# A two-block transformer on one core: scores two groups ahead of the transposes, and the window mask written into PSUM by ScalarE

## What is computed

```python
def first_block(x, ...):
    for l in range(DEPTH):                       # DEPTH = 2
        h = rmsnorm(x, norm_mix[l])
        proj = jnp.einsum('btd,de->bte', h, w_in[l])
        q, k, v, u, ug, ga, gb = jnp.split(proj, SPLITS, axis=-1)
        q = partial_rope(rmsnorm(q, q_norm[l]), cos, sin)     # 16 heads of 64
        k = partial_rope(rmsnorm(k, k_norm[l]), cos, sin)     # 2 heads of 64
        a_out = sliding_window_attention(q, k, v, sinks[l])
        c_out = conformer_conv(u, ug, conv_w[l], conv_b[l], conv_ln_g[l], conv_ln_b[l], w_conv_out[l])
        merged = jax.nn.sigmoid(ga) * a_out + jax.nn.sigmoid(gb) * c_out
        x = x + jnp.einsum('btd,de->bte', merged, w_out[l])
        h2 = rmsnorm(x, norm_ffn[l])
        gu = jnp.einsum('btd,df->btf', h2, w_gate_up[l])
        g, up = jnp.split(gu, 2, axis=-1)
        x = x + jnp.einsum('btf,fd->btd', jax.nn.silu(g) * up, w_down[l])

def sliding_window_attention(q, k, v, sinks):    # window 128, blocks of 128 queries see 256 keys
    s = jnp.einsum('bnqkgd,bnskd->bnkgqs', qb, kb) * scale
    s = jnp.where(mask, s, -jnp.inf)
    m = jnp.maximum(jnp.max(s, axis=-1, keepdims=True), sink)
    p = jnp.exp(s - m)
    p = p / (jnp.sum(p, axis=-1, keepdims=True) + jnp.exp(sink - m))
    o = jnp.einsum('bnkgqs,bnskd->bnqkgd', p, vb)
```

## Time and profile before

| | us |
|---|---|
| median of three runs | 2336.82 (2336.79 to 2336.86) |
| the profiled execution | 2334.86 |
| its span, first to last instruction | 2332.6 |
| PE busy | 2271.0 (97%) |
| DVE busy | 1137.1 (49%) |
| ACT busy | 993.5 (43%) |
| POOL busy | 981.8 (42%) |
| mean granted clock of TensorE | 0.993 of full speed |

### The profile page before, as it was taken

The page is one execution under the profiler, slowest core; times in us unless marked ns, Lnnn a source line. Parts: engine busy times, 40 slices in busy tenths (PEclk is TensorE's granted clock), DMA queues, the critical chain, the costliest instruction groups (busy, mean ns, idle before and its releaser), DMA issues.

```text
span 2332.6 us, 29198 instructions
## 1 busy us (share of the span) xinstructions
PE 2271.0 (97%) x10536; PEld 1791.9 (77%) x10560; DVE 1137.1 (49%) x1475; ACT 993.5 (43%) x1499; POOL 981.8 (42%) x453
## 2 busy tenths in 40 slices
PE   6989999999999999999999999999999999999999
PEld 5866678888888876678888888876777667888887
DVE  5876664222334785666222334647776443433300
ACT  4546643333223545744333213335535663444311
POOL 4962234444443882234444443432442113544442
PEclk9999999999999999999999999999999999999999
DMA  4321123333662221122333472322121002333332
GB/s 151 91 64 56 62 73 91 99 92 97 192 221 73 90 73 54 55 70 88 96 98 98 150 247 90 91 81 64 55 83 53 28 28 72 107 93 97 99 92 88
DMA packets 59842, 216.00 MB, mean 93 GB/s; under 512 B 6640, under 2 KB 6896, under 8 KB 59760
## 3 DMA queue, kind: packets, MB, share of 16 engines
q1 hardware_dynamic: 52272, 187.62, 26.0%
q10 hardware_dynamic: 7488, 27.27, 3.5%
HBM read 212.76 MB, written 2.10 MB: 92 GB/s over the span
## 4 chain that ended last, share of the span: by engine, by line
PE 88%; DVE 7%; ACT 4%; issue 2%; DMA 0%; SPq 0%; DVEq 0%; ACTq 0%
PE bank L1276 26%; PE bank L1278 25%; PE bank L1277 25%; PE bank L1732 1%; PE bank L1410 1%; PE bank L1289 1%; PE bank L1736 1%; PE bank L1470 1%; PE bank L1350 1%; PE bank L1450 1%; PE bank L1720 1%; PE bank L1345 1%; PE bank L1306 1%; ACT prob L479 1%; DVE root L749 1%
## 5 line engine op out<-in xcount | busy, mean ns | idle before, releaser
L307 POOL TENSOR_TENSOR wl<-raw,wh 128x1024 fp32r<-128x1024 f32 x351 | 855.7, 2438 | 1304.3 <-ACT wh L380 1304.1
L1276 PE MATMUL bank<-hh,wh 128*128 128x512 f32 x2024 | 816.3, 403 | 32.9 <-DVE hl L763 19.4
L1277 PE MATMUL bank<-hl,wh 128*128 128x512 f32 x2024 | 792.9, 392 | 0.0
L1278 PE MATMUL bank<-hh,wl 128*128 128x512 f32 x2024 | 792.8, 392 | 0.0
L380 ACT ACTIVATE wh<-raw 128x1024 fp32r<-128x1024 f32 x351 | 369.7, 1053 | 641.8 <-PE bank L1278 610.0
L1276 PEld LDWEIGHTS bank<-hh,wh 128*128 128x128 f32 x2024 | 383.1, 189 | 128.7 <-issue 28.6
L1277 PEld LDWEIGHTS bank<-hl,wh 128*128 128x128 f32 x2024 | 383.2, 189 | 86.3 <-issue 9.8
L1278 PEld LDWEIGHTS bank<-hh,wl 128*128 128x128 f32 x2024 | 382.7, 189 | 81.4
L1276 PE MATMUL bank<-ah,wh 128*128 (+1 forms) x528 | 208.0, 394 | 0.0
L1278 PE MATMUL bank<-ah,wl 128*128 (+1 forms) x528 | 207.0, 392 | 0.0
L1277 PE MATMUL bank<-al,wh 128*128 (+1 forms) x528 | 204.9, 388 | 0.0
(11 more groups left out here) (318 smaller groups left out, 2571.9 us busy)
## 6 DMA issues: line engine op xcount, KB each, us to landing
raw<-stream SPq DMA_DIRECT2D x351, 512.0 KB, 3.6
ada_w<-ada ACTq DMA_DIRECT2D x48, 512.0 KB, 4.6
x<-x_t ACTq DMA_DIRECT2D x4, 512.0 KB, 7.8
out_t<-x SPq DMA_DIRECT2D x8, 256.0 KB, 2.1
cst<-consts SPq DMA_DIRECT2D x1, 640.0 KB, 11.1
tmp<-masks SPq DMA_DIRECT2D x1, 320.0 KB, 11.3
par<-params SPq DMA_DIRECT2D x1, 253.0 KB, 4.6
cst<-consts SPq DMA_DIRECT2D x1, 224.0 KB, 8.0
```

The costliest lines, as they stand in the source:

```text
L307: nc.gpsimd.tensor_tensor(wl[:, slot, :], raw[:, raw_slot, :], wh[:, slot, :].bitcast(F32), ALU.subtract).then_inc(lo_ready, 1)
L1276: mm(dst, wh[:, slot, w], xh, start=start, stop=False)
L1277: mm(dst, wh[:, slot, w], xl, start=False, stop=False)
L1278: return mm(dst, wl[:, slot, w], xh, start=False, stop=stop)
```

## The change

The mask matmuls stay for groups 0 and 1. For groups 2 to 15 ScalarE copies `win_mask` into the two banks (`put_mask`, a new function, with a new semaphore `masked`), and the score matmuls add onto it. `put_mask(g + 4)` stands behind `exps(g + 2)`, which frees those banks.

Scores run two groups ahead: `scores(0)` and `scores(1)` stand in front of the loop, and in the loop `scores(g + 2)` stands behind the transposes of g. `maxima`, `exps` and `normalise` move with them. Gate tile 2 moves behind `scores(1)`, and gate tile 3 goes to bank 4. `SPLIT` goes from 16 to 20: four taps a layer move from VectorE to ScalarE and GpSimd. Of the layer norm the sum moves from group 4 to 3, variance from 7 to 8, root from 8 to 9, normalising and SiLU from 9 to 10, `ch` from 10 to 11, and `cl` from 10 to 12, where it now stands behind `gate`.

```diff
-        EARLY_GATES = 3
-        CO_FROM = 16 - EARLY_GATES
+        EARLY_GATES, AHEAD = 2, 2
+        CO_FROM = 13
-        TAPS_U, TAPS_Q = [2, 3, 4, 4, 4, 4], [4, 4, 3, 3, 5, 5, 5, 5]
-        SPLIT, LN_EARLY = 16, 2
+        TAPS_U, TAPS_Q = [2, 3, 4, 2, 4, 5], [5, 4, 3, 4, 5, 5, 5, 5]
+        SPLIT = 20
-        PRODUCTS_AT = {2: 3, C_K: 2, C_Q: 4, C_V: 2, C_GATE: 2, C_GATE + 1: 2, C_GATE + 2: 1}
+        PRODUCTS_AT = {2: 3, C_K: 2, C_Q: 4, C_V: 4, C_GATE: 2, C_GATE + 1: 3, C_GATE + 2: 2}
-        ADDS_AT = {2: 1, C_K: 2, C_V: 2, C_GATE: 2, C_GATE + 1: 2, C_GATE + 2: 2}
+        ADDS_AT = {2: 1, C_K: 2, C_V: 4, C_GATE: 2, C_GATE + 1: 4, C_GATE + 2: 2}
+        LN_SUM, LN_MEAN, LN_SQUARES, LN_VAR, LN_ROOT, LN_NORM, LN_HI, LN_REST = 3, 5, 6, 8, 9, 10, 11, 12
...
+                def put_mask(g):
+                    lo = P if group(g)[0] == 0 else 0
+                    b = 2 * (g % 2)
+                    act.wait_ge(exp_ready, 16 * l + g - 1)
+                    af(bank[:, b:b + 2, :].rearrange("p a (c d) -> p (a c) d", c=2)[:, :, lo:],
+                       win_mask[:, lo:2 * P].unsqueeze(1).to_broadcast([P, 4, 2 * P - lo]), ACT.Copy).then_inc(masked, 1)
...
                 exps(0)
+                exps(1)
+                put_mask(2)
+                put_mask(3)
+                gate(2)
+                products(C_GATE + 2)
+                gate(3)
...
-                    if g < 15:
-                        exps(g + 1)
+                    if g + AHEAD < 16:
+                        exps(g + AHEAD)
+                    if g + 2 * AHEAD < 16:
+                        put_mask(g + 2 * AHEAD)
...
-                    else:
-                        gate(g + EARLY_GATES)
+                    elif g:
+                        gate(g + 3)
...
-                taps(5)
-                gate(2, M_SWAP[7] % 4)
                 taps(len(own) - tapped[0])
...
                 maxima(0)
+                maxima(1)
+                gate(2, 6)
                 normalise(0)
+                normalise(1)
+                gate(3, 4)
                 for g in range(16):
...
-                    if g < 15:
-                        maxima(g + 1)
+                    if g + AHEAD < 16:
+                        maxima(g + AHEAD)
...
+                    if g + AHEAD < 16:
+                        normalise(g + AHEAD)
                     if g < CO_FROM:
-                        normalise(g + 1)
-                        if g == 12 - LN_EARLY:
+                        if g:
+                            gate(g + 3, 6)
+                        if g == LN_REST:
                             for t in range(CT):
                                 out_rest(t)
-                        gate(g + EARLY_GATES, 6)
                     else:
                         m = 2 * (g - CO_FROM)
                         gate_conv(m, 6)
...
-                        if g < 15:
-                            normalise(g + 1)
                         merge(m + 1)
...
                     if g >= 2:
-                        pe.wait_ge(exp_ready, 16 * l + g - 1)
-                    for kv in range(2):
-                        mm(bank[:, b + kv, :], ident_bf[:, :], win_mask[:, :], start=True, stop=False)
+                        pe.wait_ge(masked, 14 * l + g - 1)
+                    else:
+                        for kv in range(2):
+                            mm(bank[:, b + kv, :], ident_bf[:, :], win_mask[:, :], start=True, stop=False, skip_group_check=True)
...
                 scores(0)
-                pe.wait_ge(conv_ready, (CT - 1) * l + 2)
-                tile(c0 + C_GATE + EARLY_GATES, (c0 + C_GATE + EARLY_GATES) % RW, 6, hh, hl)
+                scores(1)
+                pe.wait_ge(conv_ready, (CT - 1) * l + 1)
+                tile(c0 + C_GATE + 2, (c0 + C_GATE + 2) % RW, 6, hh, hl)
                 pe.wait_ge(root_ready, ROOTS * l + 3)
+                tile(c0 + C_GATE + 3, (c0 + C_GATE + 3) % RW, 4, hh, hl)
...
-                    if g < 15:
-                        scores(g + 1)
                     if g >= CO_FROM:
                         out(2 * (g - CO_FROM), 6)
...
                     last.then_inc(turned, 1)
+                    if g + AHEAD < 16:
+                        scores(g + AHEAD)
```

More of the change, by code:

```diff
@@ L199, in build @@
         suffix_ready = stage("suffix_ready")
+        masked = stage("masked")
         v2_copied = stage("v2_copied")
@@ L500, in _ @@
                     af(prob_t[:, 1, :, :], bank[:, 5, :].rearrange("p (a b) -> p a b", a=4), ACT.Copy).then_inc(turned_out, 1)
-                    if g < 15:
-                        exps(g + 1)
-                    if g == 7 - LN_EARLY:
+                    if g + AHEAD < 16:
+                        exps(g + AHEAD)
+                    if g + 2 * AHEAD < 16:
+                        put_mask(g + 2 * AHEAD)
+                    if g == LN_MEAN:
                         for t in range(CT):
@@ L506, in _ @@
                             af(tmp[:, LN_TMP[t], :], conv[:, t, :], ACT.Square).then_inc(sq_ready, 1)
-                    if g == 9 - LN_EARLY:
+                    if g == LN_VAR:
                         act.wait_ge(var_out, l + 1)
                         af(root[:, :], tmp[:, 5, :], ACT.Sqrt).then_inc(root_ready, 1)
-                    if g == 11 - LN_EARLY:
+                    if g == LN_NORM:
                         for t in range(CT):
@@ L513, in _ @@
                             af(conv[:, t, :], conv[:, t, :], ACT.Silu, bias=par_l(l, "ln_b", t), scale=par_l(l, "ln_g", t)).then_inc(silu_ready, 1)
-                    if g == 12 - LN_EARLY:
+                    if g == LN_HI:
                         for t in range(CT):
@@ L946, in _ @@
                             tt(conv[:, t, :], conv[:, t, :], tmp[:, 5, :], ALU.add).then_inc(centred, 1)
-                    if g == 8 - LN_EARLY:
+                    if g == LN_SQUARES:
                         dve.wait_ge(sq_ready, l * SQ_LAYER + SQ_LN + CT)
@@ L951, in _ @@
                         tt(tmp[:, 0, :], tmp[:, 0, :], tmp[:, 4, :], ALU.add).then_inc(sq_used, CT)
-                    if g == 10 - LN_EARLY:
+                    if g == LN_ROOT:
                         invert(tmp[:, 5, :], root[:, :])
-                    if g == 11 - LN_EARLY:
+                    if g == LN_NORM:
                         for t in range(CT):
@@ L1389, in _ @@
                 pe.wait_ge(lin_free, m0 + M_SWAP[7] + 1)
-                tile(c0 + C_GATE + 2, (c0 + C_GATE + 2) % RW, M_SWAP[7] % 4, hh, hl)
                 def scores(g):
@@ L1410, in scores @@
                             last = mm(bank[:, b + kv, c + lo:c + 2 * P], q[half, 2 * j + i, n * P:n * P + P],
-                                      k[half, (n - 1) * P + lo:n * P + P], start=False, stop=i == 1)
+                                      k[half, (n - 1) * P + lo:n * P + P], start=False, stop=True, skip_group_check=True)
                     last.then_inc(scores_ready, 1)
@@ L1445, in _ @@
                     pe.wait_ge(probs_ready, 16 * l + g + 1)
-                    if g:
+                    if g == 0:
+                        pe.wait_ge(conv_ready, (CT - 1) * (l + 1))
+                    else:
                         pe.wait_ge(turned_out, 16 * l + g)
+                    if g == 1:
+                        pe.wait_ge(gate_free, 16 * l + 4)
                     for w in range(1 if n == 0 else 0, 2):
@@ L1451, in _ @@
                     last.then_inc(turned, 1)
-                    if g == 7 - LN_EARLY:
+                    if g + AHEAD < 16:
+                        scores(g + AHEAD)
+                    if g == LN_MEAN:
                         pe.wait_ge(mean_out, l + 1)
-                    if g == 9 - LN_EARLY:
+                    if g == LN_VAR:
                         pe.wait_ge(var_out, l + 1)
                     if 1 <= g < CO_FROM:
-                        pe.wait_ge(gate_free, 16 * l + g + EARLY_GATES)
-                        c = c0 + C_GATE + g + EARLY_GATES
+                        pe.wait_ge(gate_free, 16 * l + g + 3)
+                        c = c0 + C_GATE + g + 3
                         tile(c, c % RW, 6, hh, hl)
```

17 lines of the change are left out of this document (7 added, 10 removed).

## The result

The changed kernel is slower by 0.3%: 2345.06 us as the median of 14 runs, against 2338.93 for 14 runs of the kernel before beside them, a ratio of 1.003 (95% interval 1.0021 to 1.0038). That is 6.1 us; 4.2 were forecast. In time it is 2345.06 against 2341.0, inside both ranges. Half of the difference of 4.1 is the level of the kernel before (2338.9 here, 2336.8 in its first three runs), the rest is the change itself. Two executions of the kernel before, among those run beside the experiments, took 2855.57 and 5865.82 us; they are left out of the medians that follow.

A forecast was written before the change was run, and what follows sets the result against it. TensorE (PE), busy 2271.0 of 2332.6 us, was taken as the bound. Waits and clock added 9.5 us a layer, 19.0 in all, less 14.8 for masks: +4.2, so 2341.0 us, range 2330 to 2350 (the forecast's own 2335 to 2347).

The forecast's parts named there:

- output tile 1: Group 13: PE waits for gate_conv(0) behind the maxima and normalising of the scores just issued; 6.45 us, +6.2 a layer.
- start: First groups of a layer: PE waits 3.1 for group 0's values and 1.2 at gate tile 5; -1.4 a layer.
- groups 9 to 11: PE loses 0.7 to an even-chance GpSimd stall of row_max, then 1.8 to ScalarE's queue; together -0.1 a layer.
- output tile 0: Groups 12 to 13: PE waits 2.2 for the first `cl`, plus half a 1.4 stall; +2.9 a layer.
- less the waits before: The old kernel's six lines of PE waits in the attention stage, 20.1 us in all, 10.05 a layer.
- clock, less before: PE's clock halves behind the 6.45 wait at the second output tile, slowing the next tiles; +1.6 a layer, between 0 and 2.
- mask pairs: 28 pairs of mask matmuls leave PE, 14 a layer at 0.53 us each: 14.8 us less, 12.0 from below.
- Transposes behind values: On PE, eight transposes behind value matmuls take 0.85 us as behind scores, at no cost; upper end 4.7 us.
- rival 3: Transposes behind the values take 1.04, so 4.7 us of the 14.8 come back: 2345.7; chance 0.12.
- The mask write: ScalarE's 28 added mask copies: spacing 0.95 us, upper end 1.3, hidden except where ScalarE has a queue.
- Rival 1: Middle waits vanish: gate, mean, variance and first output tile are never waited for; -10 us, 2327; chance 0.2.
- Rival 2: ScalarE becomes the bound in groups 10 to 12, masks taking 1.3; 4 us a layer, 2349; chance 0.18.

The follow-up runs named there:

- the last version: Changed kernel with convolution gate, scores, products and gates reordered, two low parts behind the last gate, and a gated-attention step behind group 13's second merge: 2306.06 us, ratio 0.9857.

## Why the prediction was right, and where it was not

The time is right, and so is its main mechanism, the wait at output tile 1. The sum is less good than the time: the change is +7.8 us by the profiled stages and +6.1 by the medians, where +4.2 was forecast, and errors of both signs partly cancel in it. That it came out slower at all had a chance of only 0.5. Term by term, in us a layer (layer 0 / layer 1 where they differ):

| term | forecast | measured |
|---|---|---|
| start | 4.35 | 3.82 / 2.94 |
| mean and variance | 1.7 | 1.71 / 1.74 |
| groups 9 to 11 | 2.5 | 2.65 |
| output tile 0 | 2.9 | 2.53 |
| output tile 1 | 6.45 | 6.50 |
| less the waits before | -10.05 | -10.03 |
| clock, less before | +1.6 | +2.2 / +3.1 |
| mask pairs | -7.4 | -6.9 |
| transposes, sums of ones | 0 | +1.4 |
| sum | +2.1 | +3.9 |

1. **Masks.** By PE's timeline masks and the spacings beside them went down by 6.9 us a layer, 0.49 a pair and not 0.53. In the changed kernel's own order, leaving out 28 pairs takes 11.3 us of PE's work and not 14.8 (11.1 by the medians), since the transposes ahead of them then take 1.02 us and not 0.93.
2. **Transposes behind values** is the term whose reason failed. I took 0.85 because values are four-byte matmuls like scores; it is 1.02, part of it by what now stands behind them, which I had not looked at. So rival 3 is true in its main point, that transposes in the new place cost more, at 1.6 a layer for the transposes and 1.4 net instead of its 2.35. The row behind an output tile, which I put at the upper end, was the nearer one.
3. **The mask write** takes 1.03 us and a spacing of 0.95, as taken. But "hidden while ScalarE has room" misleads: its cost was in my walk (the start, group 10), spread over terms, and never summed. Summed it is 9.5 us, nearly all of the 11.1 that it saves. Seen so, the change has two halves of about the same size and opposite sign, beside a wait of 13 us that has nothing to do with them.
4. **The start** cost 0.5 to 1.4 less than walked. The wait of 3.1 for the first values was 2.94; the wait of 1.2 at gate tile 5 was 0.88 in layer 0 and did not appear in layer 1.
5. **Groups 9 to 11.** The half chance of the first collision was a whole one (1.18), the wait behind the table 1.47 instead of 1.8.
6. **Output tile 1.** 6.45 forecast, 6.50 twice. This wait, which follows from the order of two programs, could be added up from rows to 0.1 us.
7. **The clock** is a term of the sum that was mis-sized, by 1.1 a layer in the mean. Behind the 6.5 us it was 2.2 in layer 0 (1.6 were taken). What I had not counted are falls behind the shorter waits: 2.53 and 2.94, in layer 1. From layer 0, where 2.8 us had left the clock up, I concluded that they are free; but in layer 1 of the same profile the clock fell at the end of the same wait (at 872.4 us, for 3.4 us), which I had not read. And the tiles behind the earlier trace rows ran 2.6 us at half clock (733.3 to 735.9), not 4, so that the price of 1.9 read there was too high; the 1.6 taken was too low for the 4.9 us that the tiles of layer 0 ran at it behind the 6.50 (296.8 to 301.7).
The Trainium skill, TensorE: Matmul & The Clock Gate (section Part 1: The HAM clock gate), says that the gate's observation runs free of the kernel's start. By that rule, the trace agrees: the wait of 2.78 us fell differently in two executions of one kernel.

No run takes back the lead of two groups, the four moved taps or the moved steps of the layer norm one by one, so what each of them gives is not shown. They are held together in the run with masks back on PE.

Rival 1 is refuted, as the middle waits stayed. Rival 2's conditions did not hold (masks at 1.03), but its idea, that ScalarE's queue is what PE waits for, is what the run without masks shows.

## What to carry to other kernels

Work taken off the bounding engine and put on another is worth what is left after the second engine's queue: price both halves, by leaving the work out on both. A lead of two groups need not give slack (by the walk; no run changes it alone); what an in-order engine reads next decides, so put the result that the bounding engine waits for ahead of results that are needed two groups later. Where clock falls of 1.6 us come by chance, compare stages and many runs, and count every idle of over 1.5 us of PE as a chance of one.

## What the runs showed of the hardware

- In ten profiles, PE stood still between 2.45 and 3.17 us in 28 places of the attention stages. The clock fell behind 22 of them. Behind all six waits of 6.50 it fell, for 6.8 us, part of it still within the wait. In all fourteen profiles, it fell behind none of the 29 waits of 1.0 to 1.5 us there, and behind 10 of the 29 of 1.5 to 2.2 us, such as the 1.57 of the last version's layer 0 and not of its layer 1.
- Eight 128x128 four-byte transposes take 0.85 us between 64-row score matmuls and a tile, 1.02 between 64-column value matmuls and scores, 0.93 between values and a bf16 mask, 0.97 between an output tile and scores and 1.04 between two output tiles. Both neighbours count; why was not found.
- A ScalarE copy of 1024 columns of a bf16 mask into PSUM takes 1.03 us, against 1.05 for rounding 1024 float columns into SBUF.
- A single VectorE step of 0.68 us with two SBUF inputs took 2.83 under a GpSimd subtraction of 3.40, which itself takes 2.40 alone. Both were longer than alone.
